# S5's angles, sines, powers and input factors made in GLA's last head; adaLN tiles split four to VectorE and twelve to TensorE

## The reference, cut to what matters

```
mod   = silu(c) @ w_ada + b_ada                  # shift, scale, gate; one vector per group
h     = x * (1 + scale1) + shift1                # what the input projection reads
proj  = h @ w_in                                 # q k v r glr | u | lx ly | gates
y_lru = RG-LRU(conv(lx)) * gelu(ly)
y_gla = norm(GLA scan, 4 heads, both ways) * silu(r)
# S5, 64 groups of 64 complex states, 16 inputs each:
step  = exp(log_step);  mag = exp(lam_re * step);  ang = lam_im * step
ab    = mag * (cos(ang), sin(ang))               # one step of the state
f     = (ab - 1) / lam                           # input factor
bb    = f * b                                    # complex
s_t   = ab * s_(t-1) + bb u_t;   y_s5 = Re(c s_t) + d u
out   = merge(y_gla, y_s5, y_lru) @ w_out, layer norm, squared-ReLU MLP, layer norm
```

## Time and profile before

| | us |
|---|---|
| median of 3 runs | 2937.99 |
| lowest, highest | 2936.61, 2940.48 |
| the profiled execution | 2935.89 |
| its span in the trace | 2934.1 |
| TensorE busy, matmul | 2795.7 (95% of the span) |
| VectorE, ScalarE, GpSimd busy | 1782.6, 1137.6, 932.4 |

### The profile page before, as it was taken

The page is one execution under the profiler, slowest core; times in us unless marked ns, Lnnn a source line. Parts: engine busy times, 40 slices in busy tenths (PEclk is TensorE's granted clock), DMA queues, the critical chain, the costliest instruction groups (busy, mean ns, idle before and its releaser), DMA issues. The chain is left out here.

```text
span 2934.1 us, 41574 instructions
## 1 busy us (share of the span) xinstructions
PE 2795.7 (95%) x16768; PEld 2735.7 (93%) x16768; DVE 1782.6 (61%) x2422; ACT 1137.6 (39%) x1709; POOL 932.4 (32%) x624
## 2 busy tenths in 40 slices
PE   6999999999999998999969999999999999999996
PEld 6999998899998998999969999999999999999996
DVE  7688886364454899999954547778732223223226
ACT  2698995352643314444441101013642211211224
POOL 1334433111211265555514334333112111111223
PEclk9999999999999999999989999999999999999998
DMA  6121112011201544444443546434111111111111
GB/s 229 45 65 61 60 60 62 28 37 40 58 24 43 152 149 146 122 123 123 116 160 133 184 133 218 139 133 139 37 44 44 38 42 44 44 44 44 44 44 65
DMA packets 111179, 257.80 MB, mean 88 GB/s; under 512 B 20960, under 2 KB 54752, under 8 KB 110752
## 3 DMA queue, kind: packets, MB, share of 16 engines
q1 hardware_dynamic: 100928, 214.26, 23.3%
q10 hardware_dynamic: 10080, 41.18, 3.8%
HBM read 199.01 MB, written 56.37 MB: 87 GB/s over the span
## 5 line engine op out<-in xcount | busy, mean ns | idle before, releaser
L153 POOL TENSOR_TENSOR w_lo<-w_raw,w_hi 128x256 fp32r<-128x256 f32 x292 | 343.2, 1205 | 716.8 <-ACT w_hi L205 507.6
L2691 PE MATMUL bank<-yhi,w_hi 128*128 128x384 f32 x1560 | 525.0, 337 | 3.7 <-POOL w_lo L2621 2.3
L2691 PE MATMUL bank<-ylo,w_hi 128*128 128x384 f32 x1560 | 521.8, 335 | 0.0
L2691 PE MATMUL bank<-yhi,w_lo 128*128 128x384 f32 x1560 | 521.7, 334 | 0.0
L2621 POOL TENSOR_TENSOR w_lo<-w_raw,w_hi 128x1024 fp32r<-128x1024 f32 x69 | 169.1, 2451 | 678.4 <-ACT w_hi L2799 678.4
L2658 PE MATMUL bank<-yhi,w_hi 128*128 128x384 f32 x864 | 290.8, 337 | 27.5 <-POOL w_lo L197 22.6
L2691 PEld LDWEIGHTS bank<-yhi,w_hi 128*128 128x128 f32 x1560 | 293.2, 188 | 7.4 <-POOL w_lo L2621 3.3
L2691 PEld LDWEIGHTS bank<-ylo,w_hi 128*128 128x128 f32 x1560 | 293.4, 188 | 1.1
L2691 PEld LDWEIGHTS bank<-yhi,w_lo 128*128 128x128 f32 x1560 | 293.4, 188 | 0.0
L2658 PE MATMUL bank<-yhi,w_lo 128*128 128x384 f32 x864 | 289.6, 335 | 0.0
L2658 PE MATMUL bank<-ylo,w_hi 128*128 128x384 f32 x864 | 289.6, 335 | 0.0
(11 more groups left out here) (453 smaller groups left out, 6575.8 us busy)
## 6 DMA issues: line engine op xcount, KB each, us to landing
w_raw<-in_mlp_units SPq DMA_DIRECT2D x64, 512.0 KB, 3.6
w_raw<-in_s_units SPq DMA_DIRECT2D x32, 512.0 KB, 4.6
mrg_scr<-in_w_ada_rows SPq DMA_DIRECT2D x32, 512.0 KB, 3.7
mid_gates<-gate ACTq DMA_DIRECT2D x24, 576.0 KB, 3.3
gt<-mid_gates SPq DMA_DIRECT2D x24, 576.0 KB, 3.8
w_raw<-in_gla_units SPq DMA_DIRECT2D x25, 512.0 KB, 3.7
w_raw<-in_lru_units SPq DMA_DIRECT2D x24, 512.0 KB, 3.6
x<-in_x_t SPq DMA_DIRECT2D x16, 576.0 KB, 9.5
```

What stands on the lines that cost most here:

```text
L153: ins = pool.tensor_tensor(lo[:, part], raw[:, part], hi[:, part].bitcast(F32), ALU.subtract)
L2691: mm = pe.matmul(out, wt[SLOT[u]][:, w], r[:, k, band_cols(b)], start=(k == first and y == 0), stop=(k == last and y == 2))
```

## The change

Three things change.

1. `NROW` goes from 7 to 4: four adaLN tiles on VectorE, twelve on TensorE. The order of the loads at the start is rewritten. x_band(0, b) now waits for each `hlo` by itself, at its own k, not for all eight.
2. The S5 angles, sines, powers and input factors go into the last head of GLA: on ScalarE at the end of steps 6 and 8, on VectorE at the end of steps 7 (`angles`), 9 (`first_power`), 10 and 11 (`input_factors`), and 12 to 14 (`powers`). Their buffers are `glr` and `wgate`, which now live on into the S5 stage; `k` serves as scratch.
3. In S5 the blocks `bblk` and the outputs `yb` take over `wgate` and `glr`. VectorE zeroes the edges of `hn[1]` after states(0) rather than ahead of output_weights(0). ScalarE waits for the stores of tables 0 and 2 ahead of `decay(0)`.

```
-NROW = KD - 1
+NROW = KD // 2
 ...
-                load_row(4)
-                load_col(5)
-                load_row(5)
-                load_col(6)
-                load_pixels(3)
-                load_row(6)
-                load_pixels(4)
-                load_col(7)
+                for n in range(4):
+                    load_col(5 + n)
+                    load_pixels(3 + n)
+                load_col(9)
                 load_x(0)
-                for k in range(5, KD):
-                    load_pixels(k)
-                load_col(8)
+                load_pixels(KD - 1)
+                load_col(10)
+                load_col(11)
                 load_y(0)
 ...
                     for k in range(KD):
+                        if tiles is not None:
+                            pe.wait_ge(lo_done, tiles + k + 1)
 ...
-                    if i == 0:
-                        pe.wait_ge(lo_done, KD * (b + 1))
 ... gla, ScalarE
+                        if h == LAST and s == 6:
+                            act.wait_ge(lam_in, 16 * 6)
+                            act.wait_ge(item_mm, ITEM["gate", LAST, 1, NB - 1] + 1)
+                            act.activation(sm[0], lam[:, 2, :], ACT.Exp).then_inc(act_p, 1)
+                        if h == LAST and s == 8:
+                            act.wait_ge(trig, 1)
+                            act.activation(sm[1], sm[1], ACT.Exp).then_inc(act_p, 1)
+                            act.wait_ge(trig, 2)
+                            act.activation(sm[3], sm[2], ACT.Sin).then_inc(act_p, 1)
+                            act.activation(sm[4], sm[2], ACT.Sin, scale=0.5).then_inc(act_p, 1)
 ... gla, VectorE, last head
+                            if s == 7:
+                                angles()
+                            if s == 9:
+                                first_power()
+                            if s in (10, 11):
+                                input_factors(s - 10)
+                            if 12 <= s < 15:
+                                powers(2 ** (s - 12))
+                            if s == 15:
+                                dve.sem_inc(pw_done, 1)
 ... s5_and_gates, ScalarE
-                st(act.activation(sm[0][:], lam[:, 2, :], ACT.Exp))
-                act.wait_ge(trig, 1)
-                st(act.activation(sm[1][:], sm[1][:], ACT.Exp))
-                act.wait_ge(trig, 2)
-                st(act.activation(sm[3][:], sm[2][:], ACT.Sin))
-                st(act.activation(sm[4][:], sm[2][:], ACT.Sin, scale=0.5))
 ...
                 act.wait_ge(tab_done, 4)
+                act.wait_ge(tab_out[0], 64)
                 decay(0)
 ... s5_and_gates, VectorE: the same small operations as in the new functions go, and
-                for s in range(2):
+                def clear(s):
                     st.mark(dve.memset(hn[s][:, :, :, 0:2], 0.0))
-                    st.mark(dve.memset(hn[s][:, :, :, NCH:HN], 0.0))
-                st.sync()
+                    st(dve.memset(hn[s][:, :, :, NCH:HN], 0.0))
+                clear(0)
 ...
                     if n == 1:
                         dve.wait_ge(const_done, 1)
+                        clear(1)
```

More of the change, by code:

```diff
@@ L120, in __init__, with powers_of @@
         self.hi, self.lo = sb("gla_hi", [P, UW], F32R), sb("gla_lo", [P, UW], F32R)
+def powers_of(pre):
+    half = LAGS * GROUPS
+    pw = [pre.glr[:, c * half:(c + 1) * half].rearrange("p (l g) -> p l g", g=GROUPS) for c in range(2)]
+    flat = pre.wgate[:].rearrange("p h d -> p (h d)")
+    return pw, [flat[:, n * GROUPS:(n + 1) * GROUPS] for n in range(8)]
 class Core:
@@ L425, in _, with band @@
             def _(pe):
-                def band(u, b, out):
+                def band(u, b, out, tiles=None):
                     cols = slice(b * BW, (b + 1) * BW)
@@ L847, in gla @@
                 "rs_done", "gm_done", "rm_done", "final_done", "const_done"))
-        lam_in, u_mm = sem("lam_in"), sem("u_mm")
+        lam_in, u_mm, act_p, trig, pw_done = (sem(n) for n in ("lam_in", "u_mm", "act_p", "trig", "pw_done"))
         y_out = [sem(f"y_out{b}") for b in range(NB)]
@@ L1298, in _, with angles @@
                 st = Chain(dve, dve_s)
+                TT, TS_, STT = dve.tensor_tensor, dve.tensor_scalar, dve.scalar_tensor_tensor
+                M, A_, SB = ALU.mult, ALU.add, ALU.subtract
+                re, im = lam[:, 0, :], lam[:, 1, :]
+                s_ = sm
+                def angles():
+                    dve.wait_ge(act_p, 1)
+                    st(TT(s_[1], re, s_[0], M))
+                    dve.sem_inc(trig, 1)
+                    st(TT(s_[2], im, s_[0], M))
+                    st(TS_(s_[5], s_[2], 1 / (2 * np.pi), ROUND, M, A_))
+                    st(TS_(s_[5], s_[5], ROUND, None, SB))
+                    for cst in (C1, C2, C3):
+                        st(STT(s_[2], s_[5], -float(cst), s_[2], M, A_))
+                    st(TS_(s_[2], s_[2], 3.1415925, -3.1415925, ALU.min, ALU.max))
+                    dve.sem_inc(trig, 1)
@@ new lines, in powers @@
+                def powers(base):
+                    cnt = base
+                    pr = pw[0][:, base:base + 1, :].to_broadcast([P, cnt, GROUPS])
+                    pi = pw[1][:, base:base + 1, :].to_broadcast([P, cnt, GROUPS])
+                    xr, xi = pw[0][:, 1:1 + cnt, :], pw[1][:, 1:1 + cnt, :]
+                    orr, oi = pw[0][:, base + 1:base + 1 + cnt, :], pw[1][:, base + 1:base + 1 + cnt, :]
+                    a, b = (k[:, x * T // 2:x * T // 2 + cnt * GROUPS].rearrange("p (a g) -> p a g", g=GROUPS) for x in range(2))
+                    st.mark(TT(orr, pr, xr, M))
+                    st.mark(TT(a, pi, xi, M))
+                    st.mark(TT(oi, pr, xi, M))
+                    st(TT(b, pi, xr, M))
+                    st.mark(TT(orr, orr, a, SB))
+                    st(TT(oi, oi, b, A_))
@@ L1585, in s5_and_gates @@
         tab += [table_buffer(1)]
-        yb = [sb(f"yb{s}", [P, G4, NCH]) for s in range(2)]
+        yb = [pre.glr[:, s * G4 * NCH:(s + 1) * G4 * NCH].rearrange("p (g c) -> p g c", c=NCH) for s in range(2)]
         kst = [sb(f"kst{s}", [32, G4, KW]) for s in range(2)]
         v = sb("s5v", [P, 2, G4, NCH])
-        (p_in, act_p, trig, dve_s, pw_done, pq_done, bb_done, lag_mm, lag_done, lag_out, tab_done, tab_in0, tab_in1,
+        (p_in, dve_s, pq_done, bb_done, lag_mm, lag_done, lag_out, tab_done, tab_in0, tab_in1,
          band_done, band_free, item_done, item_free, w_done, w_free, wt_done, ca_done, pool_s, coef_done, bblk_done,
@@ L1593, in s5_and_gates @@
             sem(n) for n in (
-                "p_in", "act_p", "trig", "dve_s", "pw_done", "pq_done", "bb_done", "lag_mm", "lag_done", "lag_out",
+                "p_in", "dve_s", "pq_done", "bb_done", "lag_mm", "lag_done", "lag_out",
                 "tab_done", "tab_in0", "tab_in1", "band_done", "band_free", "item_done", "item_free", "w_done", "w_free",
```

119 lines of the change are left out of this document (49 added, 70 removed).

## The result

| | us |
|---|---|
| kernel before, median of 20 runs | 2938.02 |
| changed kernel, median of 20 runs | 2942.78 |
| ratio, changed to before | 1.0017, 95% interval 1.0011 to 1.0023 |
| changed kernel, the profiled execution | 2945.54, its span 2943.7 |

The change makes the kernel slower by 0.17%, 5.0 us by the ratio (3.2 to 6.8). The forecast was +3.7 us and 2941.7. The difference is a real one, but it lies within the 0.2% that the forecast called the same.

A forecast was written before the change was run, and what follows sets the result against it. TensorE was taken as the bound, its matmuls 2795.7 of 2934.1 us. Start +3.2, GLA's last head +0.4 and VectorE's chain in S5 +0.1 gave +3.7 on 2938.0: 2941.7 us, range 2936.5 to 2945.

The forecast's parts named there:

- The columns: Start: twelve column tiles on TensorE at 3.47 us each, bias added at 48.35 instead of 45.73, +2.6 us.
- The rival of the full clock: Start: columns run at full clock in the long stretch, bias 2.3 us earlier than before; sum -1.2 us, 2936.8; chance 0.06.
- The wait by k and the clock: Start: earlier x_band gives back 1.2 us, slow clock behind a 3.7 us wait for unit 1 takes 1.8.
- GLA's last head: Last head of GLA: `angles` delay step 8's mask from 892.54 to 892.9, +0.4 us, bounds 0 and 1.5.
- ScalarE and the other pieces: GLA's last head: ScalarE's 4.7 us fit in 5.71 idle; VectorE's other 10.7 us, spread over steps 9 to 14, are covered.
- The head start: S5: TensorE begins 4.3 us sooner but waits 9.1 instead of 4.8 us for `ub`; counted at nothing, bounds 0 and -4.3.
- the rival: S5: the head start is carried through, sum 3.7 - 4.3 = -0.6 us, 2937.4; chance 0.13.
- VectorE's chain in S5: S5: one more memory clear, about +0.1 us; GpSimd's work beside it taken as 0.
- The rival of the splits beside the unit phase: S5: two more GpSimd splits beside VectorE's 51 small operations, 1.6 us each, 3.2 more; +6.9, 2944.9; chance 0.12.

The follow-up runs named there:

- e10: e8 with the change's twelve columns, four rows and order of loads; median 2920.17 us, ratio 0.9948 to the kernel before.
- e8: Changed kernel with nine columns, seven rows, old load order, unit 1's high part earlier, x_band(0, 2) in bank 5, moves of e4 and e7; 2916.98 us, ratio 0.9928.
- e1: Kernel before with only the change's first part: twelve columns, new order of loads, wait by k; 2940.27 us, ratio 1.0006.
- e4: Changed kernel with S5's unit phase (51 small VectorE operations) moved ahead of the wait for `p_in`; 2923.61 us, ratio 0.9951 to the kernel before.
- e12: Changed kernel with the angles moved from step 7 to 9 and what follows them by up to two steps; one execution with its trace, no time given.
- e7: Changed kernel with the clearing of `hn[1]` moved behind output_weights(1); one execution with its trace, no time given.
- e2: Changed kernel without the change's first part (seven rows, nine columns, old loads, wait for eight low parts); 2939.88 us, ratio 1.0004 to the kernel before.
- e5: Kernel before with S5's unit phase (51 small VectorE operations) moved ahead of the wait for `p_in`; 2934.17 us, ratio 0.9992.
- e9: Kernel before with the wait by k alone; 2937.16 us, ratio 1.0002.
- e6: Kernel before with the wait by k, unit 1's high part made after the third `hhi`, x_band(0, 2) in bank 5; 2934.93 us, ratio 0.9993.

## Why the prediction was right, step by step

**The columns**: right to 0.1 us. 3.45 us a tile for 37.93 us without a gap, bias at 48.12 against the forecast of 48.35; with the price of the columns alone at 2.5 (e10 against e8, forecast 2.6). The rival of the full clock had asked for 43 us and has fallen. It waited for a clock that was already granted: the record reads 1.00 in the first tile too (from 5.0 to 9.0 us), and with it a two-column fp32 pass takes 0.216 us from the first tile to the last.

**The wait by k and the clock**: the mechanism right, the size too small. y_band(0, 0) waits 3.84 us (3.7 forecast) until 62.28 (62.6), but ends at 69.3, not 68.6, because the slow pace lasts 18 matmuls, where it lasted 11 in the band of 5.98 us that the prediction took for it. The shift at the wait for unit 2 is 3.9 us, 3.2 forecast, and in this execution the mis-sized term is the slow stretch. In the other traces with this start it is 10 (e1), 12 (e4), 13 (e12) and 14 (e7) matmuls. The start of before varies as well: its wait for unit 2 stands at 85.87 (before), 86.00 (e2) and 86.93 (e5), 86.3 in the mean, and that of the new start at 89.77, 88.86, 88.83, 89.10 and 89.50, 89.2 in the mean. The difference of the means is 2.9, so the forecast of 3.2 is right for the typical execution, and 3.9 belongs to the pair that was profiled. That an earlier x_band is worth nothing while y_band waits for unit 1 is shown by e9.

**GLA's last head**: +0.9 instead of +0.4, within the bounds of 0 to 1.5. The angles took 2.06 us as forecast; `queries` ahead of them began 0.36 us late against the shift of 5.33 (895.15 for 889.46), and 0.22 us stand between the last of them and the mask. ScalarE and the other pieces cost nothing, as forecast (the shift is 6.16 us at step 8 and 6.21 at the late wait). e12 shows the place. In e2 and e8, without the new start, the head costs 0.5 us, close to the forecast; the rest is the late copy of step 7, which the prediction didn't have and whose cause stays open.

**The head start**: right. 3.85 us were gained at S5's begin, and the wait for `ub` grew by 4.1. e2 excludes the rival, and e4 and e5 show the cause that the prediction named, the chain that begins at `p_in`. The prediction stopped one step short of it. It had in the earlier trace rows both the idle time ahead of `p_in` and the 17.6 us of operations behind it that need nothing from it.

**VectorE's chain in S5**: this is the term that was wrong, +0.1 forecast. The memsets were priced by their own length and not by where they push their successor (e7). Taken over all traces, lag_blocks(1) starts 182.6 us behind the end of GLA's work on TensorE in the five kernels with the old S5 (181.5 to 184.1), 184.4 us in the three that clear `hn[1]` ahead (183.0 to 185.2) and 182.0 in e7, which clears it behind: 1.8 us more, gone with the clearing moved. From the late wait of the last head to S5's last outputs it is 564.7 us (562.4 to 566.7), 567.7 (566.1 to 568.6) and 567.1: 3.0 us more, of which e7 gives back little. The shortest two of the old ones (e1, e9) wait only 2.6 us at lag_blocks(1), and there the granted clock stays at 1.00. So the term is 1.8 to 3.0 us, the clearing explains a part of it, and the rest isn't shown; the spread between kernels with one and the same S5 is larger than the difference. The rival of the splits beside the unit phase (+3.2) didn't come: from the first scaling of b to the first table VectorE takes 25.9 us before, 26.8 in the change and 25.9 in e2.

The sum of the mechanisms as the traces show them, 2.9 for the start, 0.9 for the last head and 1.8 to 3.0 for S5, is 5.6 to 6.8, in the upper part of the measured 3.2 to 6.8. The forecast of +3.7 had the signs, the start and the head start right; GLA and S5 were too low. The 4.6 us by which the two profiled executions differ beyond the measured 5.0 are of the kind that the clock rows show. Of them only the start's and S5's parts are named; the 1.2 us of the last stage are not explained.

The Trainium skill, SBUF — State Buffer, Who interferes with whom, says that a VectorE instruction with two SBUF inputs contends with a GpSimd instruction that reads SBUF. The prediction took it that this leaves open which of the two waits, but the same section says that issue order, and not the shape of the operation, decides who blocks. The changed kernel's trace agrees, from 1083.7 to 1089 us, where tiny VectorE operations, each issued just behind a GpSimd product, last as long as it does:

```profile
1083.75 1.06 POOL L1871 TENSOR_TENSOR wtmp<-pwwi,bbi 128x512 f32<-128x512 f32 x1
1083.77 1.12 DVE L2263 TENSOR_TENSOR tabt<-tabq,msw 128x32 f32<-128x32 f32 x1
1084.89 1.28 POOL L1872 TENSOR_TENSOR wtr<-wtr,wtmp 128x512 f32<-128x512 f32 x1
1084.92 1.32 DVE L2264 TENSOR_TENSOR tabq<-tabq,tabt 128x32 f32<-128x32 f32 x1
```

The same two operations take 0.20 and 0.23 us in the kernel before (1075.30 and 1075.54). The later starter waits out the other one, and the small one loses most in proportion.

## What to carry to other kernels

Work moved off the beginning of a stage is worth something only if the next thing on that engine can start: look at what its next wait stands for, and put ahead of it all that doesn't need it. Here the one edit gave 2.4 us alone (interval -0.3 to 5.0) and the other none, and both together gave 14.4 us with the slower start still in. An engine that starts earlier only to wait for another one gains nothing, and can pay for the pause with a slow clock. Price a small operation by whom it pushes beside whom, and don't read a difference of 2 us between two profiled executions as one between two kernels: from the last head to S5's last outputs the same code took 562.4 to 566.7 us here.

## What the runs showed of the hardware

The same wait of 3.69 us of TensorE is followed by a stretch at a granted clock that differs from execution to execution, 1.00, 0.72 or 0.52 over six us, with no difference in the work, and the 24 matmuls behind it take between 4.24 and 6.87 us (7.03 in e6). At lag_blocks(1) the matmuls begin at 0.50 behind waits of 4.49 to 6.93 us. In the change, after a wait of 5.77 us, the clock reads 0.85 between 3.7 and 7.7 us behind its end, and in the kernel before, after 4.52 us, 1.00. The length of the wait doesn't order this: after 4.49 us (e7) it still reads 0.50 from 4 to 6 us behind the end (1140.44 to 1142.44), and after 6.93 us (e6) 1.00 there (1137.79 to 1139.79). In the change:

```profile
1145.60:1149.60 4.00, 4.00 (x20) 4.00 (x21) 3.75 (x7) 1.55 (x5) 0.00 (x0) 0.85 0.08 18
```

In the kernel before:

```profile
1138.00:1142.00 4.00, 4.00 (x25) 4.00 (x25) 3.75 (x7) 1.43 (x5) 0.00 (x0) 1.00 0.07 16
```

VectorE and GpSimd can lengthen each other much: a GpSimd product of 512 columns took 3.10 us beside VectorE's 2048-column operations in e5 (at 1082.52), and 2.99 to 3.21 in the kernel before (1061.85 to 1067.99), against 1.05 beside its small ones in the change (1087.27). In e5 GpSimd became what TensorE waited for, 5.8 us.
